# Beta right of the triangular matrix and the state's decay on GpSimd, in a hybrid decoder layer on one core

## What is computed

```python
g = cumsum(g); decay = exp(where(tri, g_i - g_j, -inf))
lower = where(tri_strict, beta_i * (k k^T) * decay, 0)
u, w = solve(I + lower, [v * beta, k * beta * exp(g)])
qk = (q k^T) * decay
# per chunk
v_new = u - w @ state
o     = (q * exp(g)) @ state + qk @ v_new
state = state * exp(g_last) + (k * exp(g_last - g))^T @ v_new
```

## Time and profile before

| | us |
|---|---|
| median of three runs | 1242.66 |
| the profiled execution | 1242.4 |
| its span, first to last instruction | 1240.7 |
| mixer, 239.6 to 661.3 | 421.7 |
| output product, 661.3 to 753.0 | 91.7 |
| up projection, 753 to 1064 | 311 |
| down projection, from 1064 | 176.7 |
| busy in the span: PE / DVE / ACT / POOL | 1166.1 / 814.4 / 555.6 / 494.5 |

### The profile page before, as it was taken

One profiled execution on the slowest core, in us unless ns is written; L12 is line 12 of the kernel. 1 busy time (PEld: TensorE's weight loads), 2 busy tenths in 40 slices (PEclk: granted clock), 3 DMA queues, 4 the chain that ended last, 5 costly groups with the idle time before them and its releaser, 6 DMA issues.

```text
span 1240.7 us, 22379 instructions
## 1 busy us (share of the span) xinstructions
PE 1166.1 (94%) x9232; PEld 954.2 (77%) x9232; DVE 814.4 (66%) x1117; ACT 555.6 (45%) x997; POOL 494.5 (40%) x420
## 2 busy tenths in 40 slices
PE   5999999899998999999988898999999999999897
PEld 4778888887776777777766786888888888888685
DVE  5798977377888897888865653333333333767775
ACT  7444233255554535454554553333333333545443
POOL 2476246112112022021122433455454445775873
PEclk9999999899999999999988998999999999999999
DMA  7344112300000000001013353222222222564461
GB/s 243 86 136 149 65 36 60 73 23 21 21 2 21 2 22 20 2 2 36 2 52 136 119 153 99 71 68 81 73 68 70 84 68 68 165 208 136 172 235 68
DMA packets 103932, 99.82 MB, mean 80 GB/s; under 512 B 15396, under 2 KB 89368, under 8 KB 103832
## 3 DMA queue, kind: packets, MB, share of 16 engines
q1 hardware_dynamic: 102392, 93.15, 24.7%
q10 hardware_dynamic: 1440, 5.24, 1.1%
HBM read 85.24 MB, written 13.11 MB: 79 GB/s over the span
## 4 chain that ended last, share of the span: by engine, by line
PE 73%; DVE 16%; ACT 4%; issue 3%; DMA 2%; POOL 1%; SPq 1%; DVEq 0%; ACTq 0%; POOLq 0%
PE psum L1669 26%; PE psum L1961 11%; PE psum L1326 6%; PE psum L2500 6%; PE psum L1683 4%; PE psum L2540 3%; DVE arena L2383 3%; PE psum L1506 3%; PE psum L1520 2%; DVE pt_q L1221 2%; PE psum L1483 2%; PE psum L1269 1%; DVE arena L1202 1%; POOL dn_q L1839 1%; ACT pt_p L995 1%
## 5 line engine op out<-in xcount | busy, mean ns | idle before, releaser
L1669 PE MATMUL psum<-h_p,up_p 128*128 128x512 f32 x704 | 222.7, 392 | 2.4 <-DVE h_q L1658 2.4
L1669 PE MATMUL psum<-h_q,up_q 128*128 128x512 f32 x704 | 222.4, 392 | 0.0
L1800 DVE SCALAR_TENSOR_TENSOR arena<-psum,arena 128x1023 f32<-128x1023 f32 x44 | 56.5, 1283 | 198.8 <-ACT arena L1769 198.8
L1749 POOL TENSOR_TENSOR up_q<-arena,up_p 128x1024 fp32r<-128x1024 f32 x44 | 105.8, 2406 | 171.4 <-ACT up_p L1745 171.4
L1669 PEld LDWEIGHTS psum<-h_p,up_p 128*128 128x128 f32 x704 | 133.2, 189 | 30.5 <-DVE h_q L1658 2.8
L1669 PEld LDWEIGHTS psum<-h_q,up_q 128*128 128x128 f32 x704 | 133.2, 189 | 27.8
L1769 ACT ACTIVATE arena<-psum,arena 128x1024 f32<-128x1024 f32 x44 | 49.1, 1116 | 201.6 <-PE psum L1669 201.6
L1839 POOL TENSOR_TENSOR dn_q<-arena,dn_p 128x1024 fp32r<-128x1024 f32 x44 | 113.6, 2594 | 49.2 <-ACT dn_p L1835 49.2
L1855 DVE SCALAR_TENSOR_TENSOR ap_q<-ap_p,arena 128x512 fp32r<-128x512 f32 x44 | 108.7, 2498 | 37.0 <-ACT ap_p L1851 37.0
L995 ACT ACTIVATE pt_p<-psum 128x384 fp32r<-128x384 f32 x132 | 64.6, 489 | 117.7 <-PE psum L1506 117.0
L1326 PE MATMUL psum<-arena 64*64 64x64 f32 x3072 | 110.3, 221 | 4.1 <-DVE arena L1106 1.4
(11 more groups left out here) (298 smaller groups left out, 2385.6 us busy)
## 6 DMA issues: line engine op xcount, KB each, us to landing
arena<-in_ffn_w_up SPq DMA_DIRECT2D x44, 512.0 KB, 3.8
arena<-in_ffn_w_down SPq DMA_DIRECT2D x44, 512.0 KB, 3.6
arena<-in_w_in SPq DMA_DIRECT2D x20, 512.0 KB, 3.9
arena<-in_x SPq DMA_DIRECT2D x16, 512.0 KB, 5.1
qkv_mid<-arena ACTq DMA_DIRECT2D x9, 512.0 KB
arena<-qkv_mid SPq DMA_DIRECT2D x8, 576.0 KB, 4.1
arena<-in_w_out SPq DMA_DIRECT2D x8, 512.0 KB, 3.5
x_mid<-arena SPq DMA_DIRECT2D x8, 512.0 KB, 5.1
```

The costliest lines, as they stand in the source:

```text
L1669: ins = pe.matmul(up_ps[j % 2][:, g, h * 512:(h + 1) * 512], w[:, k], x[:, k, h * 512:(h + 1) * 512], start=k == 0 and x is h2_p, stop=Tru ...
L1749: pool.tensor_tensor(up_q[up_slot(u)], up_st[up_slot(u)], up_p[up_slot(u)], ALU.subtract).then_inc(late("up_lo")[0], 1)
L1800: v.scalar_tensor_tensor(out=y[:, 1:S], in0=ps[:, 0:S - 1], scalar=tap(1, u), in1=y[:, 1:S], op0=ALU.mult, op1=ALU.add).then_inc(late("up_ ...
```

## The change

In the delta rule beta moves from the rows of the system to its columns: `lower` is made from k k^T with `DTb` = `DTc` * beta, and `QTc` and `kdec` (through `ED` * beta) carry beta too. `kb`, its transpose `kbT` and its copy, `vb` and the mask `strict` go; v is copied by ScalarE (`vt`). The decay of the state moves from VectorE to GpSimd, where it is released beside the correction of v. Beside these, the mask of the selection leaves out the last block, the product of probabilities and v uses 64 columns of weights and 64 partitions of output, `ORDER` is a new string, five of the eight slices of tile 0's output product (step WP) come in the mixer, the output stage's order and buffers change and its residual is on VectorE, and the down projection has its additions and stores at other places and its last four slices (was two) tile by tile, with the last tile stored in halves.

```diff
+WO_EARLY = 5
+    "p": [("WP", k) for k in range(WO_EARLY)],
 ORDER = (
...
-    "vggtvccgstgvgvsocgtsvtsggvtvsogtvvgsctgoocvtsvtscvtwvctswvtvtsvvvttcvwtvtvtvtvtvtwcccwccvvvocwmmwmwo"
+    "gostvvggstsgmvvtggstssgcvvtggostvvgosoctsvtsgvvtgtsvtcvtvwctsvctvvtwvtvtcvwtvtvtvtcwcccppccvvwwvopmp"
+    "mwwop"
...
             def A1b(t):
-                scaled(kb, kn, beta, t).then_inc(sem("g_kq"), 1)
                 scaled(qg, qn, EG, t).then_inc(sem("g_kq"), 1)
-                pool.wait_ge(sem("g_kq"), 2 * t + 2)
-                scaled(kbg, kb, EG, t).then_inc(sem("g_kk2"), 1)
+                scaled(kg, kn, EG, t).then_inc(sem("g_kk2"), 1)
+            def B1(t, c):
+                n = 2 * t + c
+                pool.wait_ge(sem("b_vm"), n + 1)
+                pool.tensor_tensor(Sbd, Sbd, bc(EGL[:, t, c], 2, P), ALU.mult).then_inc(sem("b_dec"), 1)
...
-                pool.tensor_tensor(DTs, DTc, bc(strict, 1, GH), ALU.mult).then_inc(sem("g_DTs"), 1)
+                pool.tensor_tensor(DTb, DTc, bc(beta[:, GH * t:GH * t + GH], 2, CH), ALU.mult).then_inc(sem("g_DTb"), 1)
...
+            def A1b(t):
+                act.wait_ge(sem("g_v"), t + 1)
+                act.activation(flat(vt), psum[:, 0, 0:GDIM], ACT.Copy).then_inc(sem("g_vt"), 1)
...
-            def A1b(t):
-                v.tensor_tensor(vb, ...
-            def A2a(t):
-                v.tensor_copy(flat(kbT), psum[:, 0, 0:GDIM]).then_inc(sem("g_kbT"), 1)
...
-                then(v.tensor_tensor(Sbd, Sbd, bc(EGL[:, t, c], 2, P), ALU.mult))
             def B2(t, c):
                 v.wait_ge(sem("b_dm"), n + 1)
+                v.wait_ge(sem("b_dec"), n + 1)
...
             def A2a(t):
                 blocks(1, flat(kn), "g_t1")
-                blocks(0, flat(kb), "g_t1")
...
-                        ins = pe.matmul(o, selT[:, kv], blk_of[:, c0 * P:c1 * P], start=False, stop=True,
+                    cs = min(c1, t)
+                    if sel and cs > c0:
+                        pe.matmul(o[:, 0:(cs - c0) * P], selT[:, kv], blk_of[:, c0 * P:cs * P], start=False, stop=True, skip_group_check=True)
...
-                    ins = pe.matmul(psum[:, 7, 0:GDIM], w, p, ...
+                    ins = pe.matmul(psum[LO, 7, 0:GDIM], w[:, own_v], p, ...
...
+            def WP(k):
+                wout_product(pe, 0, [k], k == 0, False)
...
-        W_STEPS = ("P0 P1 S3 N0 P2 S5 N1 S4 H0 N2 P3 S6 H1 N3 P4 S7 H2 N4 P5 H3 N5 H4 X0 X1 H5 P6 P7 X2 N6 N7 H6 H7").split()
+        W_STEPS = ("S3 P0 P1 N0 S4 N1 H0 P2 S5 H1 N2 P3 S6 H2 N3 P4 S7 H3 N4 P5 H4 N5 X0 H5 X1 X2 P6 P7 N6 N7 H6 H7").split()
...
+            wout_product(pe, 1, range(WO_EARLY), True, False)
+            wout_product(pe, 0, range(WO_EARLY, KD), False, True)
+            wout_product(pe, 1, range(WO_EARLY, KD), False, True)
+            for t in range(2, NT - 2):
+                before = KD - 1 if t == 2 else 2
+                wout_product(pe, t, range(before), True, False)
+                turn(t - 2)
+                wout_product(pe, t, range(before, KD), False, True)
...
-            for u in range(3):
-                up_begin(u)
+            up_begin(0)
+            up_begin(1)
             turn(NT - 2)
+            up_begin(2, range(HT))
             turn(NT - 1)
+            up_begin(2, range(HT, KD))
...
-                if kk == NF + 6:
+                if kk == NF + 11:
                     stores(0)
...
                 act_split_lo(v, kk)
+                if kk in (NF + 4, NF + 5):
+                    add(2 * (kk - NF - 4) + 1)
...
+                own_k = 4 if m else 2
...
-                for k in range(NF - 2, NF):
+                for k in range(NF - own_k, NF):
                     ready(k0 + k)
                 for t in tiles:
-                    for k in range(NF - 2, NF):
+                    for k in range(NF - own_k, NF):
                         ins = pair(k0 + k, t, False, k == NF - 1)
```

More of the change, by code:

```diff
@@ L1554, in mix_split_lo, with wout_product @@
                                    op0=ALU.mult, op1=ALU.add).then_inc(sem("mx_lo"), 1)
-        W_STEPS = ("P0 P1 S3 N0 P2 S5 N1 S4 H0 N2 P3 S6 H1 N3 P4 S7 H2 N4 P5 H3 N5 H4 X0 X1 H5 P6 P7 X2 N6 N7 H6 H7").split()
+        def wout_product(pe, t, ks, first, last):
+            pe.wait_ge(sem("mx_lo"), t + 1)
+            if t >= 3 and first:
+                pe.wait_ge(*late("w_y", max(x for x in range(t) if WM_SLOT[x] == WM_SLOT[t]) + 1))
+            for k in ks:
+                if t < 2:
+                    wo_ready(pe, k)
+                for x, w in ((mix_p[mixp_of(t)], wo_p[k]), (mix_q[:, :, t * P:(t + 1) * P], wo_q[k])):
+                    for n in range(2):
+                        ins = pe.matmul(wm_ps[WM_SLOT[t]][:, n * 512:(n + 1) * 512], x[:, k], w[:, n * 512:(n + 1) * 512],
+                                        start=first and k == ks[0] and w is wo_p[k], stop=True, skip_group_check=True)
+            if last:
+                ins.then_inc(late("wo_mm")[0], 1)
+            return ins
+        WM_SLOT = (0, 1, 2, 0, 1, 0, 1, 2)
+        W_STEPS = ("S3 P0 P1 N0 S4 N1 H0 P2 S5 H1 N2 P3 S6 H2 N3 P4 S7 H3 N4 P5 H4 N5 X0 H5 X1 X2 P6 P7 N6 N7 H6 H7").split()
         W_LAST = (0, 1, 6, 3, 4, 5, 2, 7)
@@ L1673, in wout_pe @@
         def wout_pe(pe):
-            def product(t, ks, first, last):
-                pe.wait_ge(sem("mx_lo"), t + 1)
-                if t >= 3 and first:
-                    pe.wait_ge(*late("w_y", t - 2))
-                for k in ks:
-                    if t < 2:
-                        wo_ready(pe, k)
-                    for x, w in ((mix_p[mixp_of(t)], wo_p[k]), (mix_q[:, :, t * P:(t + 1) * P], wo_q[k])):
-                        for n in range(2):
-                            ins = pe.matmul(wm_ps[(t + 1) % 3][:, n * 512:(n + 1) * 512], x[:, k], w[:, n * 512:(n + 1) * 512],
-                                            start=first and k == ks[0] and w is wo_p[k], stop=True, skip_group_check=True)
-                if last:
-                    ins.then_inc(late("wo_mm")[0], 1)
-                return ins
@@ L1875, in stores @@
                 for t in range(HT * m, HT * m + HT):
[L1876 to L1880 removed]
+                    for c in range(2 if t == NT - 1 else 1):
+                        if t % 2:
+                            sp.wait_ge(sem("fin_v"), t // 2 + 1 + c)
+                        else:
+                            sp.wait_ge(*late("fin", t // 2 + 1))
+                        cols = slice(c * D // 2, (c + 1) * D // 2) if t == NT - 1 else slice(0, D)
+                        sp.dma_start(out[0, t * P:(t + 1) * P, cols], y_dn[:, t, cols]).then_inc(sem("stored"), 16)
             for kk in range(3, DN):
```

190 lines of the change are left out of this document (90 added, 100 removed).

## The result

The kernel after takes **1222.83 us** (median of 4 runs, 1222.47 to 1224.74) against 1242.84 of the kernel before beside it: 0.9835 times, 95% interval 0.9821 to 0.9849. The profiled span is 1221.1 us (before 1240.7), 19.6 us less, where 30.3 were predicted.

The account below looks back on a forecast made before the run. TensorE was taken as the bound nearly everywhere. From 1242.4 us, -2.6 - 4.4 - 1.4 - 3.3 - 3 - 14.8 - 0.8 = -30.3 gave 1212 us, range 1201 to 1230.

Parts of the forecast that it names:

- rival 4: Scan: the decay queues behind other GpSimd work each time and VectorE waits, +8 us: 1220; chance 0.08.
- Rival 1: Mixer keeps its length but for removed work; GpSimd or ScalarE waits replace VectorE's, stall near 640 returns: 1227; chance 0.20.
- The transposes of k beta: Mixer: moving beta removes three TensorE transposes per tile, 24 in all at 0.11 us each: -2.6 us.
- The stall near 640: Mixer: one slow VectorE decay at 635.14 costs TensorE 1.9 us waiting and 2.5 us slow clock: -4.4 us.
- The move of the decay at nothing: Mixer: moving the state's decay from VectorE to GpSimd was itself priced at nothing, bounds -1 and +8 us.
- The rest of the mixer: Mixer: new order and lighter VectorE cut TensorE's idle time, mostly waits for pt_q: -3 us, bounds +4 and -12.
- The narrow weights: Mixer, product of probabilities and v: 64-column weight loads are 0.05 us shorter: -3.3 us, bounds 0 and -6.6.
- rival 2: Mixer: 64-column products make TensorE drain at each shape change, 32 us, so the change is slower: 1247; chance 0.07.
- The mask without the last block: Mixer: the selection's mask skips the last block, 24 times 128 fewer columns at 0.057 us: -1.4 us.
- The output stage: Mixer's tail and output product: early slices, VectorE residual and reordered transposes remove stalls: -14.8 us, bounds -18 and -8.
- The replay: Output stage: replaying the new order with the old durations left 1.8 us of stalls.
- The down projection: Down projection: fewer stalls and a shorter end against a new 4.25 us wait: -0.8 us, bounds -6 and +4.

Follow-up runs that it names:

- b_beta: Kernel before with only beta moved to the right side of the triangular matrix: 1240.35 us, 0.9978 of before.
- b_decp: Kernel before with only the decay of the state moved from VectorE to GpSimd: 1237.65 us, 0.9955 of before.
- a_decv: Kernel after with the decay of the state back on VectorE, behind its correction of v: 1229.9 us, 0.9893 of before.
- a_ord: Kernel after with the old order of steps in the mixer, only the last 20 steps as after: 1222.39 us, 0.9823 of before.
- best: Kernel after with the old mixer order, three slices instead of four tile by tile at the end, and both norm weights loaded first: 1214.1 us, 0.9767 of before.
- a_nvwide: Kernel after with 128 columns of weights again for the products of probabilities and v: 1224.77 us, 0.9852 of before.
- a_own2: Kernel after with two slices instead of four done tile by tile at the end of the down projection: 1219.43 us, 0.9806 of before.
- a_own3: Kernel after with three slices instead of four done tile by tile at the end of the down projection: 1218.67 us, 0.9800 of before.
- best2: Kernel after, new order kept, with three slices tile by tile at the end and both norm weights loaded first: 1217.24 us, 0.9789 of before.
- a_dma: Kernel after with both norm weights of the output stage loaded ahead of the residual tiles, the second not waiting for the first: 1223.49 us, 0.9834 of before.
- a_early0: Kernel after without the five early output-product slices, tiles 0 and 1 slice by slice in turn: 1227.17 us, 0.9872 of before.

## Why the prediction was right, and where it was off

The sign and the range (1201 to 1230) held; the time was 10.7 us over the forecast by the spans (1221.1 against 1210.4). 8.1 of them are the mixer, 1.4 the down projection, 0.1 the output stage, and 1.1 lie ahead of the mixer. The measured 1222.8 is nearer to the times of rivals 4 and 1 (1220 and 1227) than to the forecast of 1212; it is the width of the range that took it in.

**The transposes of k beta (-2.6): right.** b_beta gives 2.3 to 2.7.

**The stall near 640 (-4.4): right,** in place, mechanism and size: b_decp gives 4.5 in the trace (3.6 of them behind the last scan step) and 5 to 5.6 in the time. In the new order, though, the stall is gone with the decay on VectorE too: a_decv has 9.8 us from the last step to B3, as after has. There either part of the change removes it.

**The move of the decay at nothing, -1 to +8: wrong, and by its sign.** It was priced by whether GpSimd would be late (it isn't: rival 4 is out) and the cover of the pass on VectorE was taken as whole. On VectorE it costs some 0.9 us in the old kernel outside the stall, but 6.6 in the new one, since it lies ahead of pt_q, of the step Nb and of k's norm, for which TensorE waits. In the sum this gain stands under "the rest of the mixer", where losses that were not foreseen took more than it brought.

**The rest of the mixer (-3, +4 to -12): the step that failed.** TensorE's idle time from the compression's end to the last B3 was 26.4 us before (the row below, 405.6 - 379.2) and is 29.5 after. VectorE became 14.6 us lighter (337.3 to 322.7), not 21.7, and TensorE's waits for pt_q only went from 11.6 to 10.8 us, while new waits came for the exponentials and for Nb. Up to B3, beta -2.4 and the decay -4.5 (both in the old order) and the narrow weights -1.2 (in the new one) come to -8.1, with the mask at its predicted -1.4 to -9.5; a_ord stands 9.0 below before. So the parts add up in the old order and the rest is +0.5, not -3, which is nothing that one trace of each can tell from none (best, the same mixer code as a_ord, is 1.2 us shorter there). The new order then adds 2.4 up to B3, which it gives back behind it. Rival 1 (the mixer keeps its length but for the removed work, 1227) was near in its result, not in its mechanism: other waits did take the place of those for VectorE, but not for GpSimd's decay or ScalarE's copy, for which no instruction waits in after; and the stall near 640, whose 4.4 us it gave up, did not come back.

```profile
246.50:652.10 405.60, 379.21 (x5548) 303.58 (x5548) 337.30 (x700) 208.75 (x502) 74.70 (x78) 0.99 0.06 17
```

**The narrow weights (-3.3, 0 to -6.6): size about right.** The load is 0.053 shorter, I had 0.05; two thirds of it show in the first product of a pair, and that is -3.0 us of busy time and -2 of the whole time. The Trainium skill (TensorEngine Tiling (Array Packing), Key Properties) says that a change of tiling mode drains TensorE. The rows at 612.45 and a_nvwide speak against that for weights of 64 columns over 128 rows; rival 2 is refuted.

**The mask without the last block (-1.4): not tried alone.** The line has 42 products instead of 48, in all the 24 x 128 columns fewer that were counted (24 products of 512 columns where it was 30, the shorter ones as many as before).

**The output stage (-14.8): right** (-14.7). The early slices are worth 4.6 to 5.0, where I had 4.6. The replay had 1.8 us of stalls; the trace has 1.24 and 0.93 ahead of transposes and 0.74 ahead of up products. What it didn't see is the cause of the first: two norm weights of 512 KB, the second sent for when the first has landed (the load queue of after, below). Slow clock at the start: 5 x 0.28 + 5 x 0.40 = 3.4 us at most, I had 2.7. Together these are up to 1.8 us over. Against that, the stage of a_nvwide is 1.8 us longer than that of after (399.1, 397.3): a part of the narrow weights' gain, which I had in the mixer, may be what makes this sum fit.

```profile
661.04 0.43 SPq L1621 DMA_DIRECT2D arena<-in_norm_mix_post  x1
667.87 0.33 SPq L1623 DMA_DIRECT2D arena<-in_norm_ffn_pre  x1
```

**The down projection (-0.8): sign wrong, +0.6.** The 4.25 us wait came as 4.27, in its place. The slow clock behind it costs 2.6 us, not 1.7: in the chain of waits 64 products take 17.21 us there, against 64 x 0.229 = 14.7. In the middle 1.9 to 2.3 us of waiting are left (1.88 for the product, 2.27 for its weight load, at 1148), not 1.1: VectorE's two additions, now at their new places, took 3.43 and 3.42 us, the first beside a split of weights on GpSimd and the second beside an addition and such a split; before, one of the two took 1.23 and the other, beside such a split, 3.17. The end gained 2.1, not 1.6. The chain's row, the addition and its neighbour of after, then the addition of before:

```profile
1196.84 17.21 PE psum L1990 x64
...
1142.08 3.42 DVE L1970 TENSOR_TENSOR arena<-arena 128x1024 f32<-128x1024 f32 x1
...
1141.57 2.86 POOL L1934 TENSOR_TENSOR arena<-arena 128x1024 f32<-128x1024 f32 x1
```

```profile
1144.29 1.23 DVE L1944 TENSOR_TENSOR arena<-arena 128x1024 f32<-128x1024 f32 x1
```

The Trainium skill (GPSIMD Engine Reference, Key points) states that GpSimd contends with VectorE's instructions that have two SBUF inputs, and the trace agrees (3.42 us beside GpSimd, 1.23 without). I had used that rule for the decay and not for the additions.

What stays open: the mask alone; why the exponentials and Nb come later in the new order; and the 1.1 us ahead of the mixer, where nothing was changed.

## What to carry to other kernels

A pass on the second busiest engine is not free because that engine has idle time: look at what stands behind it in its queue and whether the bound engine waits for that. Over the scan steps its price was some 0.06, 0.2 and 0.4 us for a pass of 0.56 with nothing but the work and the order around it changed, so take the move out of the finished kernel to learn its worth, not out of the old one. Removed work on the bound engine came out at two thirds of face value or more (beta all of it, the narrow weights 2 of 3 us). Work taken from VectorE came out as nothing (beta's 16 passes in the old order), as one named stall (the decay in the kernel before) or as 0.35 us a pass (the decay in the kernel after). And when slices are held back to be done tile by tile, count the buffers: with four the last buffer came free only when everything else had been done.

## What the hardware showed that I had not expected

The same code with the same order took 59.5 to 62.4 us between the compression and the first scan step, in different executions. From the first scan step to the last one, after, a_own2, a_own3 and best2 then agree within 0.07 us. But a_dma and a_early0, with the same code up to there, take 1.0 us more, all of it between the eighth and the ninth step. In both places the difference goes with the granted clock. a_own3 has 0.78 and 0.88 from 250 to 260 and 0.50 and 0.83 from 270 to 280, where after has 1.00, 1.00, 0.67 and 1.00. Between the eighth and the ninth step it is a_dma that has the low clock: after, then a_dma.

```profile
445.00:450.00 5.00, 3.44 (x59) 2.57 (x57) 4.86 (x9) 1.69 (x4) 1.34 (x2) 1.00 0.02 3
450.00:455.00 5.00, 4.51 (x88) 3.73 (x86) 4.76 (x14) 2.57 (x7) 0.00 (x0) 1.00 0.00 0
```

```profile
445.00:450.00 5.00, 3.43 (x37) 2.57 (x37) 4.83 (x10) 1.38 (x3) 0.12 (x1) 0.86 0.01 3
450.00:455.00 5.00, 5.00 (x85) 4.14 (x83) 4.14 (x12) 2.23 (x5) 0.00 (x0) 0.80 0.00 0
```

TensorE's waits ahead of it are the same in both: 1.05 us, then 0.51 and 0.52. The down projection shows it again. The wait for a weight load near 1147 is 2.27 us in after, followed by a clock of 1.00, and 2.28 us in a_dma, followed by 0.84 and 0.82, which is most of the 2.0 us that a_dma lost there. So a stage that is cut at the same instructions can be compared to a tenth of a microsecond where the whole time can't be to two, but only if its clock rows agree as well; and the same wait in the same code did not always cost the clock.
